# A decoder step's S5 scan, computed in chunks of 8 positions with Toeplitz matrices and relayouts through DRAM

## The reference: what is computed

```python
# 32 groups of 16 channels, each with 64 complex states
a_bar = exp(lam * dt);  b_bar = ((a_bar - 1) / lam) * B
bu = einsum('gph,ntgh->ntgp', b_bar, u)          # injection: 16 channels -> 64 states
bu[:, 0] += a_bar * h0                           # state handed in (zero for the prompt)
x_t = a_bar * x_{t-1} + bu_t                     # the scan, complex, along t
y = real(einsum('ghp,ntgp->ntgh', C, x)) + d * u # readout
z = gelu(y);  yc = z * sigmoid(z @ glu_w + glu_b)
# the last states of the prompt and of each sample are outputs too
```

## Time and profile before

| | |
|---|---|
| time, median of 3 runs | 1571.3 us (1566.62 to 1571.36) |
| profiled execution, span | 1566.2 us, 22651 instructions (no time of its own is given beside the span) |
| PE busy | 1374.2 us, 88% |
| DVE busy | 1137.0 us, 73% |
| ACT busy | 698.7 us, 45% |
| POOL busy | 369.1 us, 24% |
| DMA | 252.19 MB, 161 GB/s over the span |

### The profile page before, as it was taken

One profiled execution on the slowest core, in us unless ns is written; L12 is line 12 of the kernel. 1 busy time (PEld: TensorE's weight loads), 2 busy tenths in 40 slices (PEclk: granted clock), 3 DMA queues, 4 the chain that ended last, 5 costly groups with the idle time before them and its releaser, 6 DMA issues.

```text
span 1566.2 us, 22651 instructions
## 1 busy us (share of the span) xinstructions
PE 1374.2 (88%) x8610; PEld 1279.3 (82%) x8610; DVE 1137.0 (73%) x1469; ACT 698.7 (45%) x807; POOL 369.1 (24%) x444
## 2 busy tenths in 40 slices
PE   5579789899799999757978999978999999999996
PEld 4577567789799999756756788978999999999995
DVE  6998999655544454499899974544887887887884
ACT  4236232243433333323613324344676676676662
POOL 3823688400100000390377850000000000000000
PEclk9779899999899999988989999977999999999998
DMA  5123123335444445113212333523887887887870
GB/s 188 54 81 99 41 83 122 123 108 176 150 153 157 133 147 178 54 41 95 87 53 81 122 114 111 191 111 143 308 298 276 307 297 277 308 293 276 313 258 35
DMA packets 43649, 252.19 MB, mean 161 GB/s; under 512 B 5056, under 2 KB 5088, under 8 KB 31024
## 3 DMA queue, kind: packets, MB, share of 16 engines
q1 hardware_dynamic: 42048, 243.55, 44.6%
q0 software_dynamic: 1232, 6.25, 1.2%
q10 hardware_dynamic: 288, 1.31, 0.2%
HBM read 249.08 MB, written 2.02 MB: 160 GB/s over the span
## 4 chain that ended last, share of the span: by engine, by line
PE 63%; DVE 25%; issue 6%; ACT 4%; POOL 1%; DMA 1%; DVEq 0%; ACTq 0%; SPq 0%
PE bank L1606 18%; PE bank L1608 17%; PE bank L1607 17%; DVE w_lo L1037 3%; PE s_bank L1804 2%; PE bank L1618 2%; PE bank L1597 2%; ACT mw_hi L746 2%; DVE z L1256 1%; DVE z L1240 1%; DVE z L1252 1%; DVE rot_v L1240 1%; DVE z L1250 1%; DVE z L1253 1%; DVE acc L444 1%
## 5 line engine op out<-in xcount | busy, mean ns | idle before, releaser
L1043 DVE TENSOR_TENSOR mw_lo<-mraw,mw_hi 128x2816 fp32r<-128x2816 f32 x96 | 296.7, 3091 | 72.3 <-ACT mw_hi L746 64.1
L746 ACT ACTIVATE mw_hi<-mraw 128x2816 fp32r<-128x2816 f32 x96 | 245.0, 2552 | 7.5 <-PE bank L1608 7.5
L1606 PE MATMUL bank<-hn_hi,w_hi 128*128 128x320 f32 x640 | 214.7, 335 | 33.4 <-DVE w_lo L1037 20.8
L1607 PE MATMUL bank<-hn_lo,w_hi 128*128 128x320 f32 x640 | 207.5, 324 | 0.0
L1608 PE MATMUL bank<-hn_hi,w_lo 128*128 128x320 f32 x640 | 206.6, 323 | 0.0
L1037 DVE TENSOR_TENSOR w_lo<-raw,w_hi 128x1024 fp32r<-128x1024 f32 x128 | 164.2, 1298 | 21.0 <-ACT w_hi L739 19.5
L1606 PEld LDWEIGHTS bank<-hn_hi,w_hi 128*128 128x128 f32 x640 | 129.1, 202 | 59.8 <-DVE w_lo L1037 30.7
L1606 PE MATMUL bank<-mw_hi,x_hi 128*128 128x352 f32 x512 | 168.9, 330 | 1.9 <-DVE x_lo L1472 1.9
L739 ACT ACTIVATE w_hi<-raw 128x1024 fp32r<-128x1024 f32 x128 | 133.0, 1050 | 75.2 <-PE bank L1608 74.9
L1608 PE MATMUL bank<-mw_hi,x_lo 128*128 128x352 f32 x512 | 165.7, 324 | 0.0
L1607 PE MATMUL bank<-mw_lo,x_hi 128*128 128x352 f32 x512 | 165.4, 323 | 0.0
(11 more groups left out here) (377 smaller groups left out, 3392.2 us busy)
## 6 DMA issues: line engine op xcount, KB each, us to landing
mraw<-w_moe_in SPq DMA_DIRECT2D x96, 1408.0 KB, 7.8
raw<-w_in_in SPq DMA_DIRECT2D x88, 512.0 KB, 3.6
uraw<-w_gu_in SPq DMA_DIRECT2D x44, 512.0 KB, 3.5
raw<-w_br_in SPq DMA_DIRECT2D x24, 512.0 KB, 3.5
uraw<-w_dn_in SPq DMA_DIRECT2D x16, 704.0 KB, 4.1
raw<-w_wo_in SPq DMA_DIRECT2D x16, 512.0 KB, 3.5
pl<-pl_in POOLq DMA_DIRECT2D x2, 1840.0 KB, 7.5
raw<-w_glu_in SPq DMA_DIRECT2D x4, 512.0 KB, 4.8
```

The costliest lines, as they stand in the source:

```text
L746: act.activation(mw_hi[c % MSPLIT][:, :], mraw[slot][:, :], ACT.Copy).then_inc(hi_ready, 1)
L1043: dve.tensor_tensor(mw_lo[c % MSPLIT][:, :], mraw[c % MRAW][:, :], mw_hi[c % MSPLIT][:, :].bitcast(F32), ALU.subtract).then_inc(lo_ready, 1)
L1606: pe.matmul(out, w_h[k], x_h[k], start=start and k == 0, stop=False)
L1607: pe.matmul(out, w_h[k], x_l[k], start=False, stop=False)
```

## The change

S5 is no longer scanned position by position. The 320 positions become 40 chunks of 8 (32 of the prompt, one for each sample); constants `LC = 8`, `NCH = 40`, `NP = 32`. For each of the 32 groups:

- Inside a chunk the output is a lower triangular block Toeplitz matrix of 128 x 128 (8 positions x 16 channels) applied to the chunk's input (`toep`, times `drive`, whose partitions are 8 positions x 16 channels and whose columns are the chunks).
- A chunk's contribution to the state is `b_t` times `drive` (`inject`), with `b_t` made of `a_bar^j b_bar`.
- Between chunks the state is scanned over 32 columns with `a_bar^8` (`states`), two calls for 8 tiles each in place of 16 tiles of 320 positions.
- The state at the start of each chunk reaches the outputs by `cpow`, made of `C a_bar^j` (in `y_of`).

New preparation per layer: DVE makes a small table `up` of powers 0 to 8 and, once, the table `E` of 32 powers for both layers (`turns`, layer 0 only; layer 1 has neither), POOL multiplies the matrices with the powers (`powered`: `bpow` and `cpow`, in two halves of 12 operations, the second half waiting for PE's fourth transposed bank), PE transposes `bpow` (`turn(0)` ahead of slot 0, `turn(1)` in slot 1) and makes the Toeplitz kernels (`k_of`, slot 3), DVE adds `d` on their diagonal (`k_diag`). The data changes its layout through DRAM, by DMAs on ACT's queue: `u` is written after the `uc` projections and read back as `drive` in slot 5 (8 DMAs of 512 runs of 160 B); the kernels are written in slot 4 and read as `toep` in slot 9 (8 DMAs of 512 runs of 512 B); `z` is written in slot 16 and read in slot 17 (8 x 512 runs of 160 B). The GLU moves from behind slot 23 to slot 20 and its GELU to slots 12 to 15. SP's loads of the GLU's weights go behind `("gate", l, 0, 6)` and wait for `k_ready`. The transposes `bt`, ACT's `decay_of`, and POOL's work per tile are gone. POOL clears `k_scratch` in DRAM at the start by two DMAs. Some tiles lie elsewhere in SBUF: `drive` over `pl`, `bbar` and `bcomp` over the GLU's weight buffers.

The core of the diff:

```diff
@@ Plan.merge
-                if key == ("gate", l, 1, 2):
+                if key == ("gate", l, 0, 6):
                     self.order += [k for k, _ in self.loads["whole"] if k[1] == l]
@@ SP
+                    if key[0] == "glu":
+                        sync.wait_ge(k_ready, l + 1)
@@ POOL
-                powers(pool, chain, l, E_DVE, NST, xs[:, :, :, :].rearrange("p b c t -> p (b c t)"))
-                pool.sem_inc(powers_ready, 1)
+                def powered(out, of, n0, j):
+                    ...
+                    chain(pool.tensor_tensor(o_r, re, pr, ALU.mult))
+                    chain(pool.tensor_tensor(t, im, pi, ALU.mult))
+                    chain(pool.tensor_tensor(o_r, o_r, t, ALU.subtract))
+                    chain(pool.tensor_tensor(o_i, re_i, pi, ALU.mult))
+                    chain(pool.tensor_tensor(t, im_i, pr, ALU.mult))
+                    chain(pool.tensor_tensor(o_i, o_i, t, ALU.add))
+                pool.wait_ge(bbar_ready, 4 * (l + 1))
+                ...
+                for h in range(2):
+                    tiles_ = slice(NST // 2 * h, NST // 2 * h + NST // 2)
+                    n0 = l * NST + NST // 2 * h
+                    if h:
+                        pool.wait_ge(turned_full, 8 * l + 4)
+                    b_ = [bcomp[c][:, tiles_] for c in range(2)]
+                    powered([bpow[:, c] for c in range(2)], b_ + b_, n0, LC)
+                    pool.sem_inc(bpow_ready, 1)
+                    powered([cpow[:, c, tiles_] for c in range(2)], [...], n0, LC + 1)
+                    pool.sem_inc(cpow_ready, 1)
@@ ACT
+                def u_load():
+                    act.wait_ge(u_written, 16 * (l + 1))
+                    act.wait_ge(cpow_ready, 2 * (l + 1))
+                    act.wait_ge(bbar_ready, 4 * (l + 1))
+                    for t in range(LC):
+                        p0 = HG * (LC - 1 - t)
+                        act.dma_start(drive[p0:p0 + HG].rearrange("p (k g) c -> p k g c", k=KB),
+                                      u_dram[l, :, :, :, t].rearrange("g h k c -> h k g c")).then_inc(u_loaded, 16)
+                def toep_load():
+                    act.wait_ge(k_written, 16 * (l + 1))
+                    act.wait_ge(states_full, 2 * (l + 1))
+                    ...
+                def z_load():
+                    act.wait_ge(z_written, 64 * (l + 1))
+                    act.wait_ge(va_stored, 16 * (l + 1))
+                    ...
@@ DVE
-                powers(dve, chain, l, 0, E_DVE, accf, lambda w: split(l, {4: 5, 8: 5, 16: 6, 32: 6, 64: 7, 128: 8, 256: 9}[w]))
+                if l == 0:
+                    turns(lambda w: split(l, {4: 5, 8: 6, 16: 7, 32: 8}[w]))
+                    router_low()
+                else:
+                    split(l, 8)
+                def states(i):
+                    ...
+                    dve.wait_ge(states_full, 2 * l + i + 1)
+                    chain(dve.tensor_tensor(z0, v[0][:, :, 0:NP], er, ALU.mult))
+                    ...
+                    for z in (z0, z1):
+                        zf = z.rearrange("p s c -> p (s c)")
+                        chain(dve.tensor_tensor_scan(zf, d, zf, 0.0, ALU.mult, ALU.add))
+                    ...
@@ PE
+                def k_of():
+                    pe.wait_ge(cpow_ready, 2 * (l + 1))
+                    ...
+                    for s in range(NST):
+                        j, k = 32 * (s % 4), s // 4
+                        for c in range(2):
+                            mm = pe.matmul(y_bank[j:j + 32, P * k:P * k + P], bbar[:, c, s], cpow[:, c, s, 0:P], ...)
+                def inject(i):
+                    if i == 0:
+                        pe.wait_ge(turned_free, 8 * (l + 1))
+                        pe.wait_ge(u_loaded, 128 * (l + 1))
+                    else:
+                        pe.wait_ge(states_free, 2 * l + 1)
+                    for s in range(half_):
+                        for c in range(2):
+                            for g in range(2):
+                                mm = pe.matmul(s5_bank[64 * g:64 * g + 64, c, NCH * s:NCH * s + NCH],
+                                               b_t[:, c, half_ * i + s, 64 * g:64 * g + 64], drive[:, 2 * (half_ * i + s) + g], ...)
+                def y_of(ct):
+                    if ct == 0:
+                        pe.wait_ge(toep_loaded, 128 * (l + 1))
+                        ...
+                    for i in range(8):
+                        ...
+                        pe.matmul(out, toep[:, q], drive[:, q], start=True, stop=False)
+                        for c in range(2):
+                            mm = pe.matmul(out, cpow[rows_, c, s, HG:], sx[rows_, c, s], start=False, stop=c == 1)
+                turn(0)
                 for s in range(SLOT_N):
                     ...
-                    if 0 <= s - S5_AT < NST:
-                        s5_in(s - S5_AT)
-                    if 0 <= s - S5_AT - 2 < NST:
-                        s5_out_(s - S5_AT - 2)
+                    if s == ST_TRANS:          # 1
+                        turn(1)
+                    if s == ST_K:              # 3
+                        k_of()
+                    if s in (ST_INJECT, ST_INJECT + 1):   # 7, 8
+                        inject(s - ST_INJECT)
+                    if ST_Y <= s < ST_Y + KB:  # 12 to 15
+                        y_of(s - ST_Y)
+                    if s == ST_GLU:            # 20
+                        pe.wait_ge(z_loaded, 128 * (l + 1))
+                        ...
```

More of the change, by code:

```diff
@@ L200, in layer @@
             self.step(l, 1, m)
[L201 to L204, removed]
+            if m == ST_GLU - 16:
+                self.glu(l)
         for m in range(KD):
@@ L223, in layer, with glu @@
             self.reader[self.n_split - SPLIT + k] = ("v", v.n - (SPLIT - 1 - k))
+    def glu(self, l):
+        for m in range(KB):
+            self.a.take(("glu", l, m))
+            if m % 2:
+                self.loads["whole"].append((("glu", l, m // 2), ("glu", l, m)))
     def step(self, l, k, m):
@@ L328, in build @@
         uraw, cur = [], e_at
-        for i in range(URAW):
+        for i in range(URAW - 1):
             t, cur = over(f"uraw{i}", [P, UCHUNK], F32, cur)
             uraw.append(t)
-        silu, cur = over("silu", [P, 3, T], F32, cur)
         assert cur <= mix_at
+        uraw.append(sb(f"uraw{URAW - 1}", [P, UCHUNK], where=whole_at))
+        silu = sb("silu", [P, 3, T], where=w_at)
         hid_hi, cur = over("hid_hi", [P, FT, T], F32R, mix_at)
@@ L648, in _ @@
             pool.dma_start(rb[:, :], rb_in.to_broadcast([P, NEXP])).then_inc(small_loaded, 16)
+            gap = (LC - 1) * HG
+            none = cpow[:, 0, :, :].rearrange("p s n -> p (s n)")[:, 0:KB * gap].rearrange("p (k n) -> p k n", k=KB)
+            chain(pool.memset(none, 0.0))
+            for l in range(DEPTH):
+                pool.dma_start(k_dram[l, :, :, :, 0:gap].rearrange("g h k n -> (g h) k n"), none).then_inc(k_cleared, 16)
             for l in range(DEPTH):
@@ L857, in _, with turn @@
-                if l == 0:
-                    act.wait_ge(decays_done, 1)
-                decay_of(0)
-                decay_of(1)
+                def turn(h):
+                    for i in range(4 * h, 4 * h + 4):
+                        act.wait_ge(turned_full, 8 * l + i + 1)
+                        c, t0 = i % 4 // 2, 8 * h + 4 * (i % 2)
+                        act.activation(b_t[:, c, t0:t0 + 4].rearrange("p s n -> p (s n)"), s5_bank[:, i % 2], ACT.Copy)\
+                            .then_inc(turned_free, 1)
@@ L1357, in _ @@
                         y_low(ug, ya_hi[:, :, :], ya_lo[:, :, :], 1)
-                    if 0 <= tile < NST:
-                        ahead = s > 8 and s % 2 and s < SLOT_N - 1
-                        s5(tile, (lambda: split(l, upto((s - 8) // 8, s % 8) + 1)) if ahead else None)
+                    if s > 8 and s % 2 and s < SLOT_N - 1:
+                        split(l, upto((s - 8) // 8, s % 8) + 1)
+                    if s == ST_K:
+                        k_diag()
+                    if s in (ST_INJECT, ST_INJECT + 1):
+                        states(s - ST_INJECT)
+                    if s == ST_GLU + 1:
+                        glu()
+                    if s == ST_GLU + 3:
+                        for m in range(KB):
+                            y_low(yc[:, m], yc_hi[:, m], yc_lo[:, m], 3 + m)
                     if s == 0:
```

454 lines of the change are left out of this document (272 added, 182 removed).

## The result

The changed kernel takes 1600.33 us (median of 4 runs, 1598.16 to 1604.38) where the kernel before took 1571.33 in the same comparison. The ratio is 1.0197, 95% interval 1.0184 to 1.0210: 29 us slower. The forecast was 1593, 22 us slower.

A forecast was written before the change was run, and what follows sets the result against it. PE, busy 88% of the span, was taken as the bound; layer 0 at +25 (4 + 28.5 - 7.5) and layer 1 at -3 (-24 + 28.5 - 7.5) gave +22 on 1571.3, so 1593 us, range 1535 to 1645.

The forecast's parts named there:

- the likeliest case: Whole kernel: the forecast of 1593 us taken together with Rival 4, chance 0.50.
- Last xb to slot 4, +28.5: Last xb projection to slot 4, per layer: POOL's second half holds DVE's convolution, 49 us for 20.6.
- Norm to xb, -24 and +4: Norm to last xb: layer 1 loses DVE's powers, 24 us less; layer 0 gains `turns` and `up`, 4 more.
- Slot 4 to yc, -7.5: Slot 4 to the wait for yc, per layer: PE's work and new waits sum to 181 us for 188.5.
- The clock's restarts: Slot 4 to yc: granted clock falls after waits; three more restarts of 2.5 us each, 8 us a layer.
- Rival 2: DMAs of u, toep and z: small runs decide, still slower, 1657 or 1731 us; chance 0.12.
- ACT's issues: Slots: some 30 DMA issues a layer on ACT, idle 69%, counted at nothing; without cover 10 to 15 us a layer.
- `states` at 8 us: Slots: two DVE calls of about 9 us; the second holds back the splits for slot 10, 8 us.
- Rival 1: DVE not held beside POOL and u_load in 8 us, so DVE's relief decides: 1531 us, chance 0.15.
- rival 3: Half of each: contention costs POOL's 27 us only (+15), relief gives 15 a layer: 1551 us, chance 0.23.
- Rival 4: Layer 0's `turns` end 12 us later, DVE getting one operation per POOL operation: 1605 us; 0.50 together with the forecast.
- The signs: Right: slot 4 near 167 and 768, longest new waits in slots 1 to 3; wrong: `y_of` calls far from 0.23 us.

The follow-up runs named there:

- e2: Changed kernel with only POOL's order changed: cpow's second half ahead of the wait for turn(0), bpow's behind it; 1600.3 us.
- e3: Changed kernel with e2's order on POOL and turn(0) moved behind the first projection of va; 1600.4 us.
- e6: Changed kernel with POOL's tables (bpow, cpow) made by DVE between its splits, and turn(1) in slot 2; 1578.7 us.
- e8: Kernel before, with DVE's part of layer 1's powers table left out (6 of 16 tiles of E filled with a constant); 1547.6 us.
- e5: Changed kernel with each y_of call made as two calls of 64 columns, for alternate halves of the result's partitions; 1565.9 us.
- c2: c1 with y_of's calls in quarters of 32 columns, 96 calls a y_of, neighbours in different quarters; 1510.2 us.
- c4: c2 with the same 96 calls reordered, all 24 of one quarter of the result's partitions before the next; 1641.3 us.
- e7: Changed kernel with u_load, toep_load, z_store and z_load issued by POOL's queue instead of ACT's; 1580.0 us.
- c1: Changed kernel with the edits of e5, e6 and e7 together; 1528.0 us.
- e4: Changed kernel with y_of's 24 small calls placed three by three between the triples of the same slot's gate projection; 1623.0 us.

## Why the prediction was right, by its steps
**The sum.** +22 forecast, +29 measured in the medians and +33 in the stages. The direction and its reason (relief of DVE is off the path, POOL's tables are on it) held; the range and the likeliest case's own range, 1573 to 1616, hold the time. That the sum came within 7 us is partly luck: in the slots several terms were off by some 6 to 18 us a layer, in both directions.

**Last xb to slot 4, +28.5.** Measured +26 in both layers. Of its parts, the second half took 29.1 us (117.53 to 146.59), where 27 and 6 of waits were counted: POOL waits for DVE by 0.2 us an operation beside the taps, not 0.5. The convolution's last tap ended at 152.1, 35 us after POOL's start, for 36. `k_of` took 2 us and not 8. The reading that this stretch is "what the place costs" would have been wrong: e2 and e3 show that the same hold costs the same ahead of slot 0. The Trainium skill's rule (SBUF — State Buffer, section "SBUF: two separate sides") of an exclusive lock is what the taps beside POOL show, 1.9 to 2.9 us for 0.48 and 0.28 (all but one of twelve); e6 puts the price of POOL's tables over DVE's at 22 us, in an edit that also moves splits and turn(1).

**Norm to xb, -24 and +4.** Measured -23 and 0; e8 brings as much in the kernel before by itself, -25 from the norm to slot 4. In layer 0 `turns` ended at 98.5 and not at 102.

**Slot 4 to yc, -7.5: the step that failed.** It measured +3 and +1, some 20 us off over both layers, and some of its terms were off further, against each other:
- `y_of` was sized at 22 us a layer, by 0.23 a call, from small calls of 8 columns. It took 37.5 and 39.7: 0.27 to 0.3 us a call at the full clock, and the clock falls within it. Those rows had the same 128 columns of weights and 8 moving columns for 40. They could not show that the price can be avoided: the same work in narrow calls that alternate over the result's parts takes a fraction of it (e5, c2), and in another order most of that is lost again (c4).
- `inject` was sized at 12 us and took 4.1 and 5.7, `k_of` at 8 and took 2.0: there the same rows were too dear, since these calls have 64 and 32 columns of weights, and no row with such weights and few moving columns was read.
- The clock's restarts were sized at three of 2.5 us, from waits. Those came, 7 us a layer: the projections behind waits for `w_lo` took 5.2 to 6.4 us for 3.65 in layer 0. On top of them, with no term in the sum, came the restarts behind `y_of`, which has no wait: its four projections took 6.3 us each in layer 0 and 5.0 in layer 1, 11 and 5 us more. The row that the term was read from could have warned of it: the 24 products from 146.06 have no wait ahead of them. In the kernel before (columns as in the earlier trace rows) the clock falls in the small fp32 products of the gating and of S5, with two waits of 0.8 and 0.5 us between them:
```profile
141.00:144.80 3.80, 3.04 (x14) 2.26 (x15) 3.56 (x8) 3.77 (x3) 3.72 (x5) 0.90 0.45 138
144.80:146.06 1.26, 1.26 (x4) 0.34 (x2) 1.19 (x3) 1.25 (x4) 1.26 (x2) 0.50 0.00 0
```
- `u_load` was 15 us and is 3.6 and 3.1. From the first issue (171.83) to the end of PE's wait (182.35) 256 runs a DMA engine take 10.5 us, at most 0.041 each, for 0.085. The queue's own rows (columns as in the earlier trace rows; 171 to 183 us with u, 199 to 225 us with toep) give 0.028 us a packet for u and 0.077 for toep. Rival 2 (small runs decide) is out for u by a factor of three; toep's runs cost nearly the 0.085 they were sized at, and `y_of` did not wait for them.
```profile
q10 hardware_dynamic: 4224, 0.66, 62.4%
q10 hardware_dynamic: 3829, 1.90, 70.9%
```
  The Trainium skill (DMA: Bandwidth & Descriptors, section "Specifications") gives 512 B as the least transfer that reaches the line rate. The trace shows no such step: by these rows u's runs of 160 B moved 5.5 GB/s in a busy engine and toep's of 512 B 6.4, and the kernel's weight loads beside toep (288 packets, 1.05 MB, 16.3%) 15.5.
- ACT's issues were counted at nothing, 10 to 15 us without cover. The cover failed: e7 gains 12 and 10 us a layer, with what the earlier issue and a sooner return of the clock bring.
- `states` at 8 us: the waits for `w_lo` in slots 9 to 12 sum to 11.9 and 10.0 us, some of it ACT's.

**The rivals.** Rival 1 (DVE's relief decides, 1531) and rival 3 (half of each, 1551) fell on the convolution's taps and on PE's bill in the slots. Rival 4 (`turns` 12 us late) did not come, they ended at 98.5. The relief of rivals 1 and 3 is nonetheless there to be had: c1 is at 1528 once POOL, PE's calls and ACT's issues are out of its way.

**The signs.** PE's longest new waits were where they were forecast (7.2 and 8.6 us in slots 1 to 3). Slot 4 began at 160.3 for 167, and at 794.8 for 768, which leaves out layer 0's 25 us. Two signs of being wrong came true as well: calls of `y_of` at 0.27 to 0.53 us for 0.23, and DVE still what PE waits for in slots 11 and 19 (5.4 and 2.7 us).

## What to carry to other kernels
Work taken from a busy engine gains only what the critical engine waited for; before trusting a rewrite, price what it puts on the engine that ends last, by rows that agree in the width of the weights, in the moving columns and in what their neighbours are. Tables that POOL builds from SBUF were paid for by DVE in each of the places tried here, so make them on DVE where it is faster at them, or while DVE is idle. Small fp32 products did best here in narrow pieces that alternate between parts of the result's partitions, and many DMA issues on a queue that nobody waits for.

## What the runs showed that was not expected
- The same 96 calls cost 4.1 or 20.0 us by their order alone (c2, c4).
- The granted clock falls from 2.4 to 1.2 GHz with PE busy throughout (5.90 of 5.90 us at 0.50). With large products three at a time between the small calls it was 0.50 for 41.5 us and then 1.00 for 20 (e4).
- 8 DMAs of 512 runs hold ACT for 6.4 and 12.3 us (u, toep, layer 0) and POOL for 5.4 and 5.3.
- Runs of 512 B cost 2.7 times those of 160 B (0.077 and 0.028 us a packet), nearly as their bytes.
- Between two engines that keep each other out, the short operations lose: taps of 0.28 us took 2.4, POOL's 2.4 us operations stayed near 2.4 beside them.
